# QKV projections of two attention kinds in three rounded passes, and one ScalarE table for exponential and logarithm

## The reference, cut to what matters

```python
def first_block(x, ...):
    h = x
    for i in range(4):
        h = h + 0.5 * swiglu(rms_norm(h, norm_ffn1[i]), ffn1_w_gate_up[i], ffn1_w_down[i])   # D_FF 2816
        hn = rms_norm(h, norm_mix[i])
        kind, j = i % 3, i // 3
        if kind == 0:   mix = stick_breaking_attention(hn, sb_w_qkv[j], sb_w_o[j])           # layers 0, 3
        elif kind == 1: mix = moba_attention(hn, moba_w_qkv[j], moba_w_o[j])                 # layer 1
        else:           mix = mla_attention(hn, ...)                                         # layer 2
        h = h + mix
        h = h + 0.5 * swiglu(rms_norm(h, norm_ffn2[i]), ffn2_w_gate_up[i], ffn2_w_down[i])
    return rms_norm(h, final_norm)

def stick_breaking_attention(x, w_qkv, w_o):      # 16 heads of 64
    q, k, v = split(x @ w_qkv, 3)                 # [1024, 3072] weights
    z = q @ k^T * scale
    log_keep = where(past, -softplus(z), 0)
    tail = reverse_cumsum(log_keep) - log_keep
    w = where(past, exp(log_sigmoid(z) + tail), 0)
    return (w @ v) @ w_o
```

## Time and profile before

| | us |
|---|---|
| runs | 3992.7, 4003.91, 4002.61; median 4002.61 |
| the profiled execution | 3990.7 |
| its span, first to last instruction | 3988.9 |
| PE busy in the span | 3781.0 (95%) |
| DVE / ACT / POOL busy | 2164.1 / 1555.0 / 1101.1 |

### The profile page before, as it was taken

The page is one execution under the profiler, slowest core; times in us unless marked ns, Lnnn a source line. Parts: engine busy times, 40 slices in busy tenths (PEclk is TensorE's granted clock), DMA queues, the critical chain, the costliest instruction groups (busy, mean ns, idle before and its releaser), DMA issues.

```text
span 3988.9 us, 46662 instructions
## 1 busy us (share of the span) xinstructions
PE 3781.0 (95%) x17679; PEld 2987.0 (75%) x17679; DVE 2164.1 (54%) x2221; ACT 1555.0 (39%) x1935; POOL 1101.1 (28%) x574
## 2 busy tenths in 40 slices
PE   8999999999999899999999998998999998998899
PEld 6865888767888668886588786687777786686787
DVE  5644766426665356664466545336655545437554
ACT  4355444334433344344543332234343332234343
POOL 6700848305657018481065001030000001031000
PEclk9999999999999999999999999998999999998999
DMA  8634767446766157674376453201465453302463
GB/s 269 228 100 149 246 211 251 150 127 212 252 206 222 45 191 252 201 248 125 102 253 200 154 172 102 100 30 54 168 199 180 159 168 101 115 14 77 157 199 126
DMA packets 493256, 649.69 MB, mean 163 GB/s; under 512 B 16075, under 2 KB 393442, under 8 KB 493090
## 3 DMA queue, kind: packets, MB, share of 16 engines
q1 hardware_dynamic: 472356, 569.62, 44.3%
q0 software_dynamic: 19584, 75.50, 5.4%
q10 hardware_dynamic: 1150, 2.29, 0.2%
HBM read 646.29 MB, written 1.05 MB: 162 GB/s over the span
## 4 chain that ended last, share of the span: by engine, by line
issue 59%; POOLq 19%; PE 13%; POOL 7%; SPq 1%; ACT 1%; DMA 0%; DVE 0%; DVEq 0%; ACTq 0%
POOLq L602 7%; POOLq L604 6%; POOLq L606 5%; PE bank L1287 3%; PE bank L932 3%; POOL mod_zone L609 2%; POOL modrow L609 2%; PE bank L904 1%; PE bank L1423 1%; PE bank L1434 1%; POOL modrow L591 1%; POOL mod_zone L591 1%; PE bank L911 1%; PE bank L912 1%; PE bank L913 1%
## 5 line engine op out<-in xcount | busy, mean ns | idle before, releaser
L2141 DVE TENSOR_TENSOR wproj_lo<-wproj,wproj_hi 128x2048 fp32r<-128x2048 f32 x252 | 756.9, 3040 | 132.7 <-ACT wproj_hi L1671 132.7
L932 PE MATMUL bank<-wproj_hi,x_hi 128*128 128x512 f32 x2112 | 541.2, 398 | 21.8 <-DVE arena L2232 12.1
L932 PE MATMUL bank<-wproj_lo,x_hi 128*128 128x512 f32 x2112 | 534.4, 396 | 0.0
L932 PE MATMUL bank<-wproj_hi,x_lo 128*128 128x512 f32 x2112 | 526.3, 392 | 0.0
L1711 ACT CAST actT_hi<-bank 128x512 fp32r<-128x512 f32 x132 | 77.4, 587 | 1074.6 <-PE bank L959 1074.6
L932 PEld LDWEIGHTS bank<-wproj_hi,x_hi 128*128 128x128 f32 x2112 | 396.5, 190 | 117.6 <-issue 29.8
L566 POOL TENSOR_SCALAR rstd<-sumsq 128x1 f32<-128x1 f32 x38 | 7.5, 197 | 1704.9 <-ACT tok L1654 1704.7
L1671 ACT CAST wproj_hi<-wproj 128x2048 fp32r<-128x2048 f32 x252 | 469.9, 1911 | 14.5 <-DMA wproj<-in_ffn_w_gate_up 14.5
L932 PEld LDWEIGHTS bank<-wproj_hi,x_lo 128*128 128x128 f32 x2112 | 400.5, 190 | 84.7
L932 PEld LDWEIGHTS bank<-wproj_lo,x_hi 128*128 128x128 f32 x2112 | 387.6, 188 | 76.6
L904 PE MATMUL bank<-wproj,xT 128*128 128x384 f32 (+2 forms) x1216 | 421.3, 502 | 8.2 <-issue 4.7
(11 more groups left out here) (431 smaller groups left out, 5182.7 us busy)
## 6 DMA issues: line engine op xcount, KB each, us to landing
wproj<-in_ffn_w_gate_up SPq DMA_DIRECT2D x336, 512.0 KB, 6.0
wdown<-in_ffn_w_down SPq DMA_DIRECT2D x132, 1024.0 KB, 5.0
wproj<-in_ffn_w_gate SPq DMA_DIRECT2D x84, 512.0 KB, 5.0
wproj<-in_ffn_w_up SPq DMA_DIRECT2D x84, 512.0 KB, 6.6
wproj<-in_w_in SPq DMA_DIRECT2D x40, 1024.0 KB, 7.3
mod_zone<-in_mod_w POOLq DMA_DIRECT2D x36, 1024.0 KB, 6.9
modrow<-in_mod_w POOLq DMA_DIRECT2D x36, 1024.0 KB, 6.9
wproj<-in_sb_w_qkv SPq DMA_DIRECT2D x48, 512.0 KB, 5.3
```

The costliest lines, as they stand in the source:

```text
L932: last = nc.tensor.matmul(proj_ps[t][:, :], rounded(x_part[of_x](c)[:, toks]), rounded(w_part[of_w][:, c, :]), start=start and c == 0, sto ...
L2141: V.tensor_tensor(rounded(wproj_lo[w.odd][:, cols]), src[:, cols], wproj_hi[w.odd][:, cols], ALU.subtract).then_inc(cols_lo, 1)
```

## The change

The sb and moba projections get the three rounded passes that the feed-forward blocks have. The weights of a pair come in six transfers, three for each half of the 1024 rows. ACT rounds each half into `wproj_hi`; the rests of pairs 0 and 1 are made by DVE, those of pairs 2 to 7 by GpSimd. ACT rounds pair 0 at the end of feed-forward step 9, pair 1 at the end of step 10, and pair i+2 in two pieces between its instructions for pair i. x is rounded by ACT (into the upper part of the `wproj_hi` slots) and its rest taken by DVE. ACT loads the table set that has both exponential and logarithm once at the start of each sb mixer and twice in each layer of the second model; the dummy exponential goes. Only its core is shown.

```diff
+            def rest_of_pairs():                                   # GpSimd
+                for k in range(2, N_PAIRS):
+                    slot = (n.load + k) % 2
+                    for half in range(2):
+                        cols = pair_half(half)
+                        pool.wait_ge(pair_hi, 2 * (n.split + k) + 1 + half)
+                        nc.gpsimd.tensor_tensor(rounded(wproj_lo[slot][:, cols]), wproj[slot][:, cols],
+                                                wproj_hi[slot][:, cols], ALU.subtract).then_inc(pair_lo, 1)
...
+            def heads_in_halves(w_qkv):                            # SP
+                def load(i, w):
+                    room(w)
...
+                    for half in range(2):
+                        chunks = slice(half * BC, (half + 1) * BC)
+                        for s in range(3):
+                            sp.dma_start(dst[:, chunks, s], src[:, chunks, s, bass.ds(i.n(P), P)]
+                                         ).then_inc(pair_in[w.odd][half], DMA)
...
+                def project_in_halves(i, w, t, mid):               # TensorE
...
+                    if k == 0:
+                        pe.wait_ge(x_rounded, 4 * n.entries + 2 * (t + 1))
+                    for c in range(KC):
+                        if t == 0 and c % BC == 0:
+                            pe.wait_ge(pair_hi, 2 * (n.split + k) + 1 + c // BC)
+                        if mid is not None and c == BC:
+                            mid()
+                        nc.tensor.matmul(proj_ps[t][:, 0:384], rounded(pair_x_hi(c)[:, toks]), rounded(hi[:, c, :]),
+                                         start=(c == 0), stop=False, skip_group_check=True)
+                    if k == 0:
+                        x_here(t)
+                    for c in range(KC):
+                        nc.tensor.matmul(... rounded(x_lo[:, c, toks]), rounded(hi[:, c, :]) ...)
+                    for c in range(KC):
+                        if t == 0 and c % BC == 0:
+                            weights_rest(c // BC)
+                        last = nc.tensor.matmul(... rounded(pair_x_hi(c)[:, toks]), rounded(lo[:, c, :]) ...)
+                    last.then_inc(proj_done, 1)
...
+            def round_pair(i, w, parts=range(2)):                  # ScalarE
+                for half in parts:
+                    act.wait_ge(pair_in[w.odd][half], i.half(3 * DMA, 3 * DMA))
+                    cols = pair_half(half)                         # 1536 columns
+                    nc.scalar.copy(rounded(wproj_hi[w.odd][:, cols]), wproj[w.odd][:, cols]).then_inc(pair_hi, 1)
...
                     if k + 2 < FF_STEPS or k + 2 == FF_STEPS and ffn_next:
                         round_columns(st.plus(2), w.plus(2))
+                    if k + 2 >= FF_STEPS and pairs_next:
+                        round_pair(Step(n.split + k + 2 - FF_STEPS), w.plus(2))
...
                         nc.scalar.activation(soft[:, hd], soft[:, hd], ACT.Ln, bias=1.0).then_inc(sb_soft, 1)
-                    nc.scalar.activation(table_pick[:, :], minus_half[:, 0:1], ACT.Exp)
...
                     if kind == "sb":
                         softplus_tails(i, u)
+                        if ahead_pair:
+                            round_pair(split_pair, w.plus(2), [0])
                         if more:
                             evac(i.plus(1), w.plus(1), 0)
                         if k:
                             copy_outputs(i.plus(-1), c.plus(-1))
                         exp_arg(i, u, 0)
+                        if ahead_pair:
+                            round_pair(split_pair, w.plus(2), [1])
                         if more:
                             evac(i.plus(1), w.plus(1), 1)
...
                     weights(i, 0)
                     weights(i, 1)
+                    if ahead_pair:
+                        round_pair(split_pair, w.plus(2), [0])
                     if k + ahead < pairs:
                         evac(i.plus(ahead), w.plus(ahead), 0)
                     if k and kind != "diff":
                         copy_outputs(i.plus(-1), c.plus(-1))
+                    if ahead_pair:
+                        round_pair(split_pair, w.plus(2), [1])
...
+                if kind == "sb":
+                    nc.scalar.preload_act_table_set("natural_log_exp_and_others")
...
+            def rest_of_pair(i, w):                                # VectorE, pair 0 in step 9, pair 1 after x
+                for half in range(2):
+                    cols = pair_half(half)
+                    v.wait_ge(pair_hi, 2 * i + 1 + half)
+                    V.tensor_tensor(rounded(wproj_lo[w % 2][:, cols]), wproj[w % 2][:, cols], wproj_hi[w % 2][:, cols],
+                                    ALU.subtract).then_inc(pair_lo_first, 1)
```

More of the change, by code:

```diff
@@ L153, in __init__ @@
         self.rows = 0
+        self.entries = 0
+        self.split = 0
     def dmas(self, w, per):
@@ L335, in x_hi, with pair_x_hi, pair_half @@
             return x_hi_parts[c // BC][:, c % BC, :]
+        pair_x_hi_parts = [wproj_hi[i][:, PAIR_COLS:KC * 512].rearrange("p (c s) -> p c s", s=SEQ) for i in range(2)]
+        def pair_x_hi(c):
+            return pair_x_hi_parts[c // BC][:, c % BC, :]
+        def pair_half(half):
+            return slice(half * PAIR_COLS // 2, (half + 1) * PAIR_COLS // 2)
         gate = sb("gate", [P, NT, 512])
@@ L408, in program @@
         cols_hi, cols_lo = sem("cols_hi"), sem("cols_lo")
+        pair_in = [[sem(f"pair_in{odd}_{half}") for half in range(2)] for odd in range(2)]
+        pair_hi, pair_lo_first, pair_lo = sem("pair_hi"), sem("pair_lo_first"), sem("pair_lo")
         rows_rounded, rows_lo = sem("rows_hi"), sem("rows_lo")
@@ L1037, in attend @@
                 heads_cat = kind == "mla"
+                in_halves = kind in ("sb", "moba")
                 dk = MLA_QH if heads_cat else DH
@@ L1151, in out_chunks @@
                     if t == 0:
-                        pe.wait_ge(w_in[w.odd], DMA * (n.landed[w.odd] + (2 if kind == "mla" else 3) * pairs // 2 + 2))
+                        pe.wait_ge(w_in[w.odd], DMA * (n.landed[w.odd] + (2 if kind == "mla" else 0) * pairs // 2 + 2))
                     rhs = wproj[w.odd][:, :].rearrange("p (c n) -> p c n", c=KC)
@@ L1238, in attend @@
                 n.pair += pairs
-                n.loaded(pairs, 2 if kind == "mla" else 3)
+                n.loaded(pairs, {"mla": 2, "diff": 3}.get(kind, 0))
+                if in_halves:
+                    n.entries += 1
+                    n.split += pairs
                 if kind == "diff":
@@ L1804, in pair @@
                     more = k != pairs - 1
+                    ahead_pair = k + 2 < pairs and kind in ("sb", "moba")
+                    split_pair = Step(n.split + i.s - n.pair + 2, i.j)
                     if kind == "sb":
                         softplus_tails(i, u)
+                        if ahead_pair:
+                            round_pair(split_pair, w.plus(2), [0])
                         if more:
@@ L1846, in attend @@
                 n.load += pairs
+                if kind in ("sb", "moba"):
+                    n.split += pairs
                 if kind == "sb":
@@ L2217, in copy_even, with ffn @@
                 n.odd += (kc + 1) // 2 // 2
-            def ffn(ffn_next, then, row=None, rows={}, layer=None, behind={}, begun=None):
+            def ffn(ffn_next, then, row=None, rows={}, layer=None, behind={}, begun=None, pairs_next=False):
                 scaled = row is not None
@@ L2243, in step @@
                         rest_of_columns(st.plus(2), w.plus(2))
+                    if k + 2 == FF_STEPS and pairs_next:
+                        rest_of_pair(n.split, n.load + FF_STEPS)
                     if k in rows:
@@ L2977 @@
 ARENA = 20224
+PAIR_COLS = KC * 384
 CONSTANTS_END = 11712
```

80 lines of the change are left out of this document (57 added, 23 removed).

## The result

The changed kernel takes 4030.93 us (median of 5 runs, 4025.39 to 4039.31), the kernel before 3994.76 (5 runs, 3986.06 to 4003.91). The ratio is 1.0094, with a 95% interval of 1.0080 to 1.0108. Forecast were 4011 us against 4002.61, a ratio of 1.002, with chances of 39% for "slower" and 38% for "the same". The measured time lies outside the 4004 to 4018 us given for that forecast and inside the wide range of all cases, 3970 to 4038. The profiled execution of the changed kernel has a span of 4037.6 us, 48.7 above the one before; it belongs to the slowest of its runs.

The account below looks back on a forecast made before the run. TensorE was taken to set the pace, busy 3781.0 of 3988.9 us. Terms 18.6 - 3.2 - 3.2 + 7.0 - 5.9 - 2.6 - 2.6 = +8.1 us gave 4011 us against the median 4002.61; range 3970 to 4038.

Parts of the forecast that it names:

- the likeliest case: Whole kernel: the summed terms give +8.1 us, 4011 us against 4002.61, own range 4004 to 4018; chance 0.40.
- The passes: Projections: 48 rounded matmuls of 174 ns replace 16 full-precision ones, 1.98 us less a pair, gross gain 47.5 us.
- The term for pair 6: Pair 6's stretch, no rounding beside it, gains the full 1.98 us; three layers, -5.9 us.
- The first tail: Feed-forward end before the mixer: rounding pair 0 delays step 10, last down products 6.2 us late; three layers, +18.6 us.
- Entering the mixer: Mixer start: first pair gains 1.98 less 0.9 us waiting for hid, about 1.05; three layers, -3.2 us.
- A middle sb pair: Middle sb pairs: GpSimd's subtraction holds head 0's tensor_tensor, 15.4 in place of 15.66 us; 12 pairs, -3.2 us.
- rival A: Sb pairs: the other turn at the port holds head 1's chain too, 17.5 us a pair, 4036 us; chance 0.22.
- A middle moba pair: Middle moba pairs: rotary tensor_tensors held by GpSimd, 16.4 in place of 15.25 us; 6 pairs, +7.0 us.
- The rest: Includes the last sb pair, whose open chain gains a table load of 1.28 us; two layers, -2.6 us.
- B: Middle pairs: no exclusion worth the name between GpSimd and VectorE, full 1.98 us gained, 3971 us; chance 0.17.
- C: Tails: pair 0's half lands early enough, no stall, 18.6 us fall, 3992 us; chance 0.13.
- D: Pairs: table loads stay in the loop or shorter matmuls still take 228 ns, about 4036 us; chance 0.08.

Follow-up runs that it names:

- tail_filled: Changed kernel plus 18 unused rounded matmuls of 512 columns before the waiting transposes in the tails of layers 0, 1 and 3; 4023.1 us, ratio 1.0078 to before.
- pairs_filled: Changed kernel plus unused rounded matmuls before the turning of queries and keys, 6 per sb pair and 12 per moba pair (pairs 0 to 5); 4012.12 us, 1.0040.
- tail_late: Changed kernel with pair 0's ScalarE roundings moved behind step 10's own work, VectorE's rests split around tile 0's residual; 4003.89 us, ratio 1.0021 to before.
- tables_only: Kernel before with only the table part: one load per sb mixer, two per layer of the second model, no dummy exponential; 3983.13 us, ratio 0.9976.
- both: Changed kernel with pair 0's roundings behind step 10's work and the rests of pairs 2 to 7 made by VectorE; 3944.29 us, ratio 0.9871 to before.
- passes_only: Changed kernel with table loads and dummy exponential kept as before; 4060.38 us, ratio 1.0167 to before.

## Why the prediction was wrong

The forecast of the likeliest case was no measurable change; the kernel became slower by 0.94%. By the prediction's own steps:

- **The passes: right.** Forecast 174 ns a matmul and 1.98 us a pair. Rows show 174 ns, and in layer 0 the stretch of pair 6, with no rounding beside it, is 14.70 us (337.36 to 352.06) after 16.62 (321.92 to 338.54): 1.92 less. The term for pair 6 was still too good: layer 1 gained 0.86 there (14.40 after 15.26) and layer 3 lost 0.11 (16.73 after 16.62), since half-clock stretches begun in pair 5 reach into it. In all -2.7 us in place of -5.9.
- **The first tail: chain right, wait and cost wrong.** ScalarE and VectorE were as late as forecast (6.05 us, 6.2 forecast), but TensorE stood for 4.3, 4.1 and 5.4 us, at its transposes, and not 6.2 before the last down products. Even so the term, 18.6 us for three layers, measured 25.7: 15.0 of idle and 10.6 of slower work. tail_filled has 16.7 with the clock nearly kept, near the forecast's term, so some 9 us are the half-clock stretches.
- **Entering the mixer: right in sb.** 14.43 us (213.66 to 228.09) became 13.54 (223.20 to 236.74): 0.9 less, 1.05 forecast. In moba it grew from 15.53 to 15.85 us: TensorE waits there for the rotary instructions, 2.15 us (to 795.98) where it waited 1.77, and the clock falls behind that. In all -1.5 us in place of -3.2.
- **A middle sb pair: chain right, time wrong.** In 11 of the 12 pairs the turns are those that the prediction took, tensor_tensor of head 0 held, head 1 not. The first pair of layer 3 took rival A's second turn: head 1's is held too, and the pair took 20.0 us. pairs_filled has 15.2 to 15.3 us for all of its steady pairs, not 17.5; its first pairs take 16.8 and 18.7 (the latter again with both heads held). The term was -3.2 us for 12 pairs and measured +14.4. Head 1 in layer 3's first pair:

```profile
1908.41 3.70 DVE L2493 TENSOR_TENSOR arena<-arena 128x512 f32<-128x512 f32 x1
```

- **A middle moba pair: chain nearly right, total in part by luck.** +7.0 forecast, +8.1 measured. The rotary instructions are held, but by less than forecast in four of the six pairs: the first, of 64 columns, takes 1.25 us (810.58 to 811.83), in the others 1.05 to 3.04, and TensorE waits for the last of them 0.7 to 2.67 us. With the filler six pairs take 97.2 us, 4.3 more than before; without it 101.0. So about 3.8 of the 8.1 us are clock, which the forecast had at nothing, and the hold alone costs less than the 7.0: the forecast's pair (16.4) was 0.2 us too long, and the 15.25 that it was set against is under the mean of the six pairs before, 15.49.
- **The rest: small.** The last sb pair gained 0.7 us in layer 0 (10.62 after 11.31) and 1.7 in layer 3 (10.40 after 12.11), half-clock stretches included: 2.4 in place of 2.6.

The step that failed is one that the prediction does not write down as a step: it prices each of TensorE's waits at its own length ("6.2 us late", "15.4 in place of 15.66") and carries the clock of the earlier trace rows, 1.00, into a kernel with new waits. So the term of the sb pairs, -3.2 us, measured +14.4, and that of the tails, 18.6, measured 25.7. With waits of 0.9 to 5.4 us came half-clock stretches of 3.4 to 13.7 us, in the tails and in the mixers. Where the filler kept TensorE at work, the same chains gave nearly the forecast's numbers (16.7 for 18.6, 93.05 for 92.4, 97.2 for 98.4).

The account is of one profiled execution of each kernel. These two are 48.7 us apart, 40.6 more than the 8.1 forecast: 17.6 in the sb pairs, 7.1 in the tails, 1.1 in the moba pairs, 6.8 in the rest of the three mixers and 8 elsewhere (the unchanged mixer of layer 2 alone is 6.4 longer). The medians are only 36 apart, a miss of 28: the profiled execution of the changed kernel is its slowest. Which of the terms are smaller in a median execution is not known.

The sign of the pair was in reach. A cut of 1.98 us from TensorE's busy time that is followed by a chain of the same length turns into idle time. The trace before held the price as well: in its last sb pair TensorE waits 2.17 us to 347.51 and is granted half its clock from 348.8 on (the earlier trace rows has 0.95 for that stretch), and the same pair of 64-column matmuls takes 0.64 us after 0.39:

```profile
347.51 0.55 PE L1105 MATMUL bank<-ident,arena 128*128 128x128 f32 x3 [2.17 <-ACT arena L1790]
...
348.06 0.39 PE L1122 MATMUL bank<-arena 128*128 128x64 f32 x2
...
348.99 0.64 PE L1122 MATMUL bank<-arena 128*128 128x64 f32 x2
```

The rivals: B fell (two-input VectorE instructions are held until GpSimd's ends), C fell for this kernel, and tail_late shows what it would have been worth (0.7%); D fell, no load is left inside a pair; A's second turn came in one pair of twelve, not in all. That A's 4036 us lies near the measured time is no support for it: the time came from the clock.

## What to carry to other kernels

Price a new wait of TensorE as its length plus what the clock can take around and after it, and read in the trace before what the matmuls behind a wait of that length did; where a chain sets the pace, work taken off TensorE turns into such waits. An idle GpSimd is no free helper while VectorE carries a critical chain: its two-input subtraction held one VectorE instruction until it was done (3.85 us in place of 0.69), while VectorE itself had room for the work. What the next phase needs belongs behind the engine's last instruction of this one, or that instruction waits for the next phase's DMA.

## What the hardware showed that was not expected

- With a wait of 4.31 us came 10.2 us at 1.2 GHz, in the mixers with waits of 0.9 to 2.7 us 3.4 to 13.7. But the length of the wait does not decide it. In layer 0 of pairs_filled the same first wait of 2.19 us (to 246.76) has 6 matmuls of 512 columns right behind it, and no half-clock stretch follows; in layer 3 the same wait, with the same 6 matmuls behind it, has 3.4 us at half clock from 1894.45 on. A wait of 2.04 us in layer 0 of tables_only (to 345.29) is followed by none, the same wait in its layer 3 (to 1972.01) by one. The waits of 0.67 to 0.79 us in the sb mixer of layer 0 of `both`, five before the last pair, were followed by none, nor were waits of 0.68 and 0.84 us in the changed kernel's moba pairs (to 829.99 and 864.46). What decides between these is not settled here.

```profile
1894.70 0.90 PE L1187 MATMUL bank<-ident,arena 128*128 128x128 f32 x3 [2.19 <-ACT arena L1890]
...
345.29 0.55 PE L1105 MATMUL bank<-ident,arena 128*128 128x128 f32 x3 [2.04 <-ACT arena L1789]
```

- Busy time rises as the clock falls: 3781.0 us before, 3793.0 after, 3736.7 in `both`, which has the same matmuls as the changed kernel. The rise after the change is half clock, not work.
- A VectorE scan, too, is held: in passes_only GpSimd's subtraction starts at 247.03 and one scan at 247.07 takes 3.95 us; without it two take 1.27. The prediction had left this open.

```profile
247.03 7.20 POOL L637 TENSOR_TENSOR wproj_lo<-wproj,wproj_hi 128x1536 fp32r<-128x1536 f32 x2 [14.82 <-ACT wproj_hi L1763]
...
247.07 3.95 DVE L2487 TENSOR_TENSOR_SCAN arena<-ones,arena 128x256 f32<-128x256 f32 x1
```
